# An expert layer over 256 tokens: 64 tokens by gathered rows, 192 by dense stages

## The chip, the cores and the metric

The kernel runs on one core of a Trainium2 chip. The metric is the device time of one execution in microseconds (us). The kernel before takes 3086.05 us (median of 3 runs, 3082.75 to 3087.93).

## What is computed

Two transformer blocks over 256 tokens of width 2048, in float32. The last layer is what the change touches: a product-key expert layer ("PEER"). Each of 8 heads of a token picks its 16 best of 16384 experts, so a token has 128 experts with a gate each; an expert is one row of `w_u` and one row of `w_v`, both of 2048 values.

```python
experts = e1 * PEER_KEYS + e2
gates = jax.nn.softmax(sc, axis=-1).astype(h.dtype)
...
    u = jnp.take(w_u, ib, axis=0)
    a = jnp.einsum('td,tkd->tk', hb, u)
    c = gb * jax.nn.gelu(a)
    vv = jnp.take(w_v, ib, axis=0)
    return jnp.einsum('tk,tkd->td', c, vv)
```

Its result is added to x, and a last RMS norm with a gain gives the output.

## The kernel before

Each engine has its own program, and semaphores join them. All weights come in items of 1 MB (128 partitions of 2048 values): SP loads item n into one of four slots of `raw` (L621) once item n-4 has been used; ScalarE rounds it to `w_hi` (L1361); VectorE subtracts to get `w_lo` (L2071); TensorE multiplies high and low parts, in the rounded format fp32r. Both splits run two items ahead of the matmuls.

The expert layer doesn't gather. It computes all 16384 experts for all 256 tokens and weighs them with a dense matrix of gates that is zero for experts not chosen. An item holds 128 experts. The experts are in four quarters of 32 items, and the stages follow each other as U0, U1, V0, U2, V1, U3, V2, V3; U is the product with `w_u`, V that with `w_v`.

- U0 (`activations`, L1220, q = 0): per item 16 blocks of 3 matmuls of 256 columns (the tokens). Meanwhile VectorE's `choose` (L2772) finds each token's experts.
- U1, U2, U3: per item 16 blocks of one matmul of 512 columns (high and low part of the tokens side by side, L1228) and one of 256 (L1232). VectorE adds the two halves (`add_halves`, L2905), ScalarE applies gelu (L1923), VectorE multiplies with the gates (`weigh_item`, L2899).
- U1 also makes the gates, 8 tokens per item: VectorE builds one-hot rows (`hots`, L2871 to L2878), TensorE multiplies them (`dense`, L1255), VectorE uses one quarter's gates (`weigh`, L2886), ScalarE keeps the other three (`keep`, L1935), and its queue sends them to memory (L1939). `fetch` brings them back in V0 and V1.
- V (`outputs`, L1259): per item 8 PSUM banks (2 halves of the tokens, 4 pieces of 512 columns), 3 matmuls of 512 columns each (L1274 to L1276). The stationary operand is the weighed activations of 128 tokens, as `c_hi` (ScalarE, L1955) and `c_lo` (VectorE, L2911). `c_hi` of an item waits until the item two before it has been used.

In V VectorE's order per item is `low_c` of the next item, then `split` of the one after it. In the tail VectorE adds the eight banks to x (L3006), ScalarE squares and sums (L2036), VectorE and ScalarE find the norm, and VectorE, ScalarE and GpSimd (L2057, its only work in the kernel) scale and send.

## Time and profile before

| | us |
|---|---|
| median of 3 runs | 3086.05 |
| shortest and longest run | 3082.75, 3087.93 |
| span of the profiled execution, first to last instruction | 3082.7 |
| expert stages, U0 to V3, within the span | 1600.7 to 3072.8 |

No time of the profiled execution is given beside its span; the span is within 0.1 us of the shortest run. In the rows below, PE is TensorE's matmuls, PEld its weight loads, DVE VectorE, ACT ScalarE, POOL GpSimd, SP the load queue; ACTq and SPq are queues that issue. A matmul's duration holds its way through the array, and matmuls overlap, so what one costs in a stream is the distance between two starts.

### The profile page before, as it was taken

The numbers are of one execution on the slowest core, as the hardware profiler recorded it, in microseconds if no ns is written. First come the engines' busy times: TensorE is split into PE (matmuls) and PEld (weight loads), VectorE is DVE, ScalarE is ACT, GpSimd is POOL, SyncE is SP. The second block draws the span as 40 slices with busy tenths as digits, with TensorE's granted clock in tenths as the row PEclk, the third lists the DMA queues.
The fourth block names the chain that finished last, engine by engine and source line by source line (L and its number), as shares of the span: only waits on it lengthen the run. The fifth ranks groups of instructions, "written<-read, shape, count | busy, mean of one in ns | idle before, by whom it ended". The sixth has DMA issues, their size and how long they took to land. (4 is left out here: it accounts for less than half of the span.)

```text
span 3082.7 us, 41075 instructions
## 1 busy us (share of the span) xinstructions
PE 2982.3 (97%) x16258; PEld 2568.4 (83%) x16258; DVE 1906.9 (62%) x2375; ACT 1360.0 (44%) x1511; POOL 5.3 (0%) x8
## 2 busy tenths in 40 slices
PE   7999989899998999999999999999999999999998
PEld 6888777789887888877899988878888888888887
DVE  4656675656586545464579988846565455554454
ACT  4544454444445443345535444444434443344444
POOL 0000000000000000000000000000000000000000
PEclk9999999999999999999999999999999999999999
DMA  6555534245453555444444555566555655555554
GB/s 240 180 196 186 194 131 174 73 168 182 153 194 108 178 184 189 154 158 155 141 163 180 188 186 206 206 235 226 213 187 203 232 193 188 190 191 191 206 195 157
DMA packets 97138, 560.56 MB, mean 182 GB/s; under 512 B 10888, under 2 KB 26880, under 8 KB 35328
## 3 DMA queue, kind: packets, MB, share of 16 engines
q1 hardware_dynamic: 73152, 522.03, 48.1%
q10 hardware_dynamic: 23872, 36.95, 3.4%
q8 instruction: 79, 1.29, 0.2%
q14 instruction: 35, 0.29, 0.0%
HBM read 543.15 MB, written 15.73 MB: 181 GB/s over the span
## 5 line engine op out<-in xcount | busy, mean ns | idle before, releaser
L2071 DVE TENSOR_TENSOR w_lo<-raw,w_hi 128x2048 fp32r<-128x2048 f32 (+2 forms) x500 | 1128.1, 2261 | 670.6 <-ACT w_hi L1361 664.8
L1361 ACT ACTIVATE w_hi<-raw 128x2048 fp32r<-128x2048 f32 (+2 forms) x500 | 940.8, 1888 | 397.8 <-DMA raw<-in_w_in_2.0 93.2
L767 PE MATMUL ps<-w_hi,hT 128*128 128x512 f32 (+3 forms) x1344 | 519.4, 386 | 12.0 <-DVE w_lo L2071 11.5
L769 PE MATMUL ps<-w_hi,hT 128*128 128x512 f32 (+3 forms) x1344 | 512.6, 381 | 0.0
L768 PE MATMUL ps<-w_lo,hT 128*128 128x512 f32 (+3 forms) x1344 | 512.4, 381 | 0.0
L1228 PE MATMUL ps<-hT,w_hi 128*128 128x512 f32 x1536 | 485.0, 397 | 0.5 <-issue 0.5
L1274 PE MATMUL ps<-w_hi,c_hi 128*128 128x512 f32 x1024 | 399.1, 390 | 4.0 <-DVE c_lo L2911 4.0
L1276 PE MATMUL ps<-w_hi,c_lo 128*128 128x512 f32 x1024 | 399.1, 390 | 0.0
L1275 PE MATMUL ps<-w_lo,c_hi 128*128 128x512 f32 x1024 | 399.0, 390 | 0.0
L1232 PEld LDWEIGHTS ps<-hT,w_lo 128*128 128x128 f32 x1536 | 288.6, 188 | 68.2
L767 PEld LDWEIGHTS ps<-w_hi,hT 128*128 128x128 f32 x1344 | 253.5, 189 | 59.5 <-DVE w_lo L2071 8.5
L1232 PE MATMUL ps<-hT,w_lo 128*128 128x256 f32 x1536 | 301.7, 278 | 0.0
L769 PEld LDWEIGHTS ps<-w_hi,hT 128*128 128x128 f32 x1344 | 253.5, 189 | 45.6
L768 PEld LDWEIGHTS ps<-w_lo,hT 128*128 128x128 f32 x1344 | 253.6, 189 | 44.0
L1228 PEld LDWEIGHTS ps<-hT,w_hi 128*128 128x128 f32 x1536 | 233.7, 189 | 0.9 <-issue 0.7
L1274 PEld LDWEIGHTS ps<-w_hi,c_hi 128*128 128x128 f32 x1024 | 192.6, 188 | 44.6 <-issue 3.7
L1276 PEld LDWEIGHTS ps<-w_hi,c_lo 128*128 128x128 f32 x1024 | 192.6, 188 | 40.0
L1275 PEld LDWEIGHTS ps<-w_lo,c_hi 128*128 128x128 f32 x1024 | 192.5, 188 | 40.0
L1955 ACT ACTIVATE c_hi<-work 128x256 fp32r (+1 forms) x128 | 53.4, 417 | 367.1 <-PE ps L1276 360.1
L1923 ACT ACTIVATE work<-work (+1 forms) x96 | 40.1, 418 | 318.4 <-DVE work L2905 318.4
L825 PE MATMUL ps<-w_hi,hT 128*128 128x512 f32 x384 | 154.5, 402 | 10.8 <-DVE hT L2174 10.6
L826 PE MATMUL ps<-w_lo,hT 128*128 128x512 f32 x384 | 152.0, 396 | 0.0
(274 smaller groups left out, 3418.3 us busy)
## 6 DMA issues: line engine op xcount, KB each, us to landing
raw<-in_w_u_t SPq DMA_DIRECT2D x128, 1024.0 KB, 4.8
raw<-in_w_v SPq DMA_DIRECT2D x128, 1024.0 KB, 5.3
raw<-in_w_in_2.0 SPq DMA_DIRECT2D x32, 1024.0 KB, 4.7
raw<-in_odd_w.0 SPq DMA_DIRECT2D x20, 1024.0 KB, 4.8
raw<-in_even_w.3608 SPq DMA_DIRECT2D x16, 1024.0 KB, 4.8
raw<-in_w_out.0 SPq DMA_DIRECT2D x16, 1024.0 KB, 4.8
raw<-in_w_out.1 SPq DMA_DIRECT2D x16, 1024.0 KB, 4.8
raw<-in_w_out_2.0 SPq DMA_DIRECT2D x16, 1024.0 KB, 4.8
```

What stands on the lines that cost most here:

```text
L767: pe.matmul(o, hi, wh, start=(j + k == 0), stop=False)
L768: pe.matmul(o, hi, wl, start=False, stop=False)
L769: mm = pe.matmul(o, lo, wh, start=False, stop=(j == 3 and k == 3))
L825: pe.matmul(o, hi, wh, start=begins and k == 0, stop=False)
L826: pe.matmul(o, hi, wl, start=False, stop=False)
L1228: pe.matmul(ps[:, s % 2, :], w_hi[:, s, k * P:(k + 1) * P], hT[:, k].rearrange("p n t -> p (n t)"), start=(k == 0), stop=False, skip_group ...
L1232: mm = pe.matmul(ps[:, s % 2, 0:S], w_lo[:, s, k * P:(k + 1) * P], hT_hi[:, k], start=False, stop=(k == KC - 1), skip_group_check=True)
L1274: pe.matmul(o, ch, wh, start=first and b in fresh, stop=False, skip_group_check=True)
L1275: pe.matmul(o, ch, wl, start=False, stop=False, skip_group_check=True)
L1276: mm = pe.matmul(o, cl, wh, start=False, stop=last and b in ends, skip_group_check=True)
L1361: act.activation(w_hi[:, s, 0:size], raw[:, s, 0:size], ACT.Copy).then_inc(hi_done, 1)
L2071: dve.tensor_tensor(w_lo[:, s, 0:size], raw[:, s, 0:size], w_hi[:, s, 0:size].bitcast(F32), ALU.subtract).then_inc(lo_done, 1)
```

## The change

Tokens 192 to 255 leave the dense expert stages. Their experts are gathered: GpSimd issues 128 indirect DMAs, each of 128 rows of 8 KB (two experts for each of the 64 tokens, one per partition), 64 from `w_u` and then 64 from `w_v`, into two buffers. VectorE multiplies each U row with the token's h and sums it, ScalarE applies gelu once to all, and VectorE adds each V row, weighed, to `YSUM`. Both run inside the loops of V0 to V3, 16 to 26 rows to a stage (`ROW_SHARE`). `YSUM` lies in the columns of `hT` that the 64 tokens leave.

The dense stages and the gates are for 192 tokens: U matmuls have 384 and 192 columns (192 in U0), the gates take 24 steps instead of 32. In V, the banks of the second half now hold 64 tokens only; their high and low parts lie side by side as one stationary operand of 128 columns, so two matmuls do instead of three. The two halves of such a bank, and `YSUM`, are joined at the end by f32 matmuls with a matrix of ones at pairs (`PAIRS`). VectorE's loops of these stages are written out instead of looped. The core of the diff:

```diff
+SG = 64
+SD = S - SG
...
+    c_parts = sb("c_parts", [P, 2, 2 * S], F32R)
+    c_hi, c_lo = c_parts[:, :, 0:S], c_parts[:, :, S:2 * S]
...
+    ROWS = [W(22880, D), W(18432, D)]
+    HROW, GROW = W(20832, D), W(22880, D)
+    YSUM = gaps[:, :, :, SD:S].rearrange("p k n t -> p (k n) t")
+    N_U, N_ROWS = P * SG // P, 2 * P * SG // P
+    PAIRS = W(20480, 2, P)
...
+                both_parts = ps[:, s % 2, 0:2 * SD].rearrange("p (n t) -> p n t", n=2)
                 for k0 in range(0, KC, 2):
                     for k in (k0, k0 + 1):
-                        pe.matmul(ps[:, s % 2, :], w_hi[:, s, k * P:(k + 1) * P],
-                                  hT[:, k].rearrange("p n t -> p (n t)"), start=(k == 0), stop=False,
-                                  skip_group_check=True)
+                        pe.matmul(both_parts, w_hi[:, s, k * P:(k + 1) * P], hT[:, k, :, 0:SD], start=(k == 0),
+                                  stop=False, skip_group_check=True)
                     for k in (k0, k0 + 1):
-                        mm = pe.matmul(ps[:, s % 2, 0:S], w_lo[:, s, k * P:(k + 1) * P], hT_hi[:, k], start=False,
-                                       stop=(k == KC - 1), skip_group_check=True)
+                        mm = pe.matmul(ps[:, s % 2, 0:SD], w_lo[:, s, k * P:(k + 1) * P], hT_hi[:, k, 0:SD],
+                                       start=False, stop=(k == KC - 1), skip_group_check=True)
                 mm.then_inc(item_used, 1)
...
+            banks = (2, 3, 4, 5, 6, 7, 0, 1) if first else END_BANKS if last and q > LASTU else range(8)
...
+                if b < 4:
+                    ch, cl = c_hi[:, s % 2, 0:P], c_lo[:, s % 2, 0:P]
+                    pe.matmul(o, ch, wh, start=begins, stop=False, skip_group_check=True)
+                    pe.matmul(o, ch, wl, start=False, stop=False, skip_group_check=True)
+                    mm = pe.matmul(o, cl, wh, start=False, stop=ends_, skip_group_check=True)
+                else:
+                    c2 = c_parts[:, s % 2, P:S]
+                    pe.matmul(o, c2, wh, start=begins, stop=False, skip_group_check=True)
+                    mm = pe.matmul(o, c2, wl, start=False, stop=ends_, skip_group_check=True)
...
+        with pe.Fori(0, STEPS // RAW) as i:
             for s in range(RAW):
                 activations(i, s, 1)
                 dense(i, s)
-        for s in range(RAW - 1):
-            activations(LOOPS - 1, s, 1)
-            dense(LOOPS - 1, s)
-        dense(LOOPS - 1, RAW - 1)
-        activations(LOOPS - 1, RAW - 1, 1)
+        with pe.Fori(STEPS // RAW, LOOPS) as i:
+            for s in range(RAW):
+                activations(i, s, 1)
         for q in range(PARTS):
...
+        pe.wait_ge(fin_in, 32)
+        pe.wait_ge(row_used, N_ROWS)
+        for n in range(4):
+            pe.wait_ge(fin_add, n + 1)
+            pe.matmul(ps[:, 4 + n, :], PAIRS[:, 0], x[:, 1, n * 512:(n + 1) * 512], start=True, stop=False)
+            pe.matmul(ps[:, 4 + n, :].rearrange("p (a t) -> p a t", t=SG), PAIRS[:, 1], YSUM[:, 8 * n:8 * n + 8],
+                      start=False, stop=True).then_inc(joined, 1)
...
+        pool.wait_ge(h_ready, 1)
+        pool.dma_start(HROW[0:SG], HROW[SG:P]).then_inc(h_in, 16)
+        pool.wait_ge(evac_act, pq_act0 + 4)
+        pool.tensor_copy(YSUM[SG:P], x[SG:P, 1].rearrange("p (a t) -> p a t", t=SG)).then_inc(y_set, 1)
+        pool.memset(YSUM[0:SG], 0.0).then_inc(y_set, 1)
+        pool.wait_ge(y_set, 2)
+        pool.memset(x[SG:P, 1], 0.0).then_inc(y_set, 1)
+        pool.wait_ge(picked, 2)
+        pool.dma_start(gsm[0:SG, 0], gsm[SG:P, 2]).then_inc(pick_in, 16)
+        pool.wait_ge(pick_in, 16)
+        for n in range(N_ROWS):
+            if n == 1:
+                for b in range(2):
+                    pool.wait_ge(gates_out[b], 16 + 16 * STEPS // 2)
+            if n >= 2:
+                pool.wait_ge(row_used, n - 1)
+            k = n % N_U
+            pool.indirect_dma_start(ROWS[n % 2], None, A["w_u_rows"] if n < N_U else A["w_v_2"][0],
+                                    bass.IndirectOffsetOnAxis(ap=PICKS[:, k:k + 1].bitcast(U32), axis=0)
+                                    ).then_inc(row_in[n % 2], 16)
+        pool.wait_ge(fin_in, 32)
+        for b in range(2):
...
+            c = CTS[q % 2][:, 4 * i + s]
+            dve.tensor_tensor(c_lo[:, s % 2, 0:P], c[:, 0:P], c_hi[:, s % 2, 0:P].bitcast(F32), ALU.subtract)
+            dve.tensor_tensor(c_parts[:, s % 2, SD:S], c[:, P:SD], c_hi[:, s % 2, P:SD].bitcast(F32), ALU.subtract
+                              ).then_inc(c_lo_done, 1)
...
+        def rows():
+
+            dve.wait_ge(h_in, 16)
+            for n in range(N_U):
+                dve.wait_ge(row_in[n % 2], 16 * (n // 2 + 1))
+                dve.tensor_tensor_reduce(ROWS[n % 2], ROWS[n % 2], HROW, 1.0, 0.0, ALU.mult, ALU.add,
+                                         AROW[:, n:n + 1]).then_inc(row_used, 1)
+                yield
+            dve.wait_ge(row_gelu, 1)
+            dve.tensor_tensor(CROW, CROW, PICK_OF, ALU.mult).then_inc(row_c, 1)
+            dve.wait_ge(row_c, 1)
+            dve.wait_ge(y_set, 3)
+            for n in range(N_U, N_ROWS):
+                dve.wait_ge(row_in[n % 2], 16 * (n // 2 + 1))
+                dve.wait_ge(row_used, n)
+                dve.scalar_tensor_tensor(out=YSUM, in0=ROWS[n % 2].rearrange("p (a t) -> p a t", t=SG),
+                                         scalar=CROW[:, n - N_U:n - N_U + 1], in1=YSUM, op0=ALU.mult, op1=ALU.add
+                                         ).then_inc(row_used, 1)
+                yield
+
+        rowing = rows()
+        ROW_SHARE = {("V", 0): 24, ("U", 2): 16, ("V", 1): 24, ("U", 3): 16, ("V", 2): 26, ("V", 3): 22}
+
+        def take_rows(part, m):
+
+            n, of = ROW_SHARE[part], QTR - 2
+            for _ in range(min(m + 1, of) * n // of - min(m, of) * n // of):
+                next(rowing)
 
         def weave():
 
-            def step(i, s, last=False):
-                ends = last and s == RAW - 1
-                if not ends:
...
+            hots(0)
+            for m in range(QTR):
+                i, s = m // RAW, m % RAW
+                if m + 1 < STEPS:
+                    hots(m + 1)
                 u_split(i, s, 1)
...
+                if m < STEPS:
...
+            for m in range(QTR):
+                i, s = m // RAW, m % RAW
                 u_split(i, s, q)
...
+                take_rows(("U", q), m)
...
+            for m in range(QTR):
+                i, s = m // RAW, m % RAW
+                v_step(i, s, i == LOOPS - 1)
+                if q == 0 and 3 <= i < 5:
+                    if m == 3 * RAW:
+                        dve.wait_ge(gates_in, 16 * PIECES)
+                        dve.wait_ge(gelu_done, 2 + 2 * QTR)
+                    weigh_four(i - 3, s)
+                take_rows(("V", q), m)
...
+        def joined_gain(n):
+            dve.wait_ge(fin_sum, 4 + n + 1)
+            dve.tensor_tensor(XG1[:, n * 512:(n + 1) * 512], ps[:, 4 + n, :], GFIN[:, n * 512:(n + 1) * 512], ALU.mult
+                              ).then_inc(fin_g, 1)```

Left out are the smaller shapes of the gate tables, the order of the banks in the last item (4 to 7 first), the tail's order of sums, two more loads (`GROW`, `PAIRS`) on ScalarE's queue, and this, early in the key projection on VectorE:

```diff
+                if g == 0 and j == 3:
+                    dve.scalar_tensor_tensor(out=HROW[SG:P], in0=x[SG:P, 1], scalar=sm(NR + 1)[SG:P], in1=GROW[SG:P],
+                                             op0=ALU.mult, op1=ALU.mult).then_inc(h_ready, 1)
...
+            if q == PARTS - 1:
+                act.wait_ge(row_used, N_U)
+                act.activation(CROW, AROW, ACT.Gelu_apprx_tanh).then_inc(row_gelu, 1)
```

## Rows read from the trace of the kernel before

**Rows 1.** Page, part 1: busy time, share of span, instructions.

```profile
PE 2982.3 (97%) x16258; PEld 2568.4 (83%) x16258; DVE 1906.9 (62%) x2375; ACT 1360.0 (44%) x1511; POOL 5.3 (0%) x8
```

**Rows 2.** Stages U0 to V3, tail: stretch, length, busy by engine, clock, DMA share, GB/s.

```profile
1600.70:1786.40 185.70, 185.22 (x1542) 184.99 (x1542) 164.68 (x334) 93.90 (x83) 0.00 (x0) 1.00 0.49 176
1786.40:2017.30 230.90, 224.97 (x1792) 200.55 (x1792) 199.51 (x203) 97.38 (x96) 0.00 (x0) 1.00 0.58 201
2017.30:2193.20 175.90, 175.82 (x769) 145.42 (x770) 96.85 (x74) 73.25 (x65) 0.00 (x0) 0.99 0.68 237
2193.20:2371.90 178.70, 178.48 (x1026) 155.59 (x1024) 105.24 (x95) 70.97 (x64) 0.00 (x0) 1.00 0.53 188
2371.90:2546.00 174.10, 174.10 (x768) 144.16 (x769) 89.06 (x68) 72.00 (x65) 0.00 (x0) 1.00 0.63 217
2546.00:2724.60 178.60, 178.59 (x1026) 155.63 (x1024) 105.00 (x94) 71.16 (x64) 0.00 (x0) 1.00 0.53 188
2724.60:2898.50 173.90, 173.69 (x766) 143.88 (x767) 88.01 (x68) 71.61 (x65) 0.00 (x0) 1.00 0.55 194
2898.50:3072.80 174.30, 174.30 (x770) 144.33 (x769) 86.44 (x70) 72.79 (x73) 3.38 (x3) 1.00 0.52 180
3072.80:3082.70 9.90, 0.41 (x2) 0.00 (x0) 4.37 (x9) 4.63 (x11) 1.71 (x2) 0.69 0.52 212
```

**Rows 3.** Waits in V1: who waited for whom, us, times, longest.

```profile
ACT c_hi L1955 <- PE ps L1276: 92.9, 30, 3.3
DVE w_lo L2071 <- ACT w_hi L1361: 42.0, 31, 2.3
```

**Rows 4.** Timelines (start, duration); by-line rows (durations min/median/max): V0, U0, f32.

```profile
2185.69 0.39 PE L1274 MATMUL ps<-w_hi,c_hi 128*128 128x512 f32 x1
...
2192.95 0.39 PE L1276 MATMUL ps<-w_hi,c_lo 128*128 128x512 f32 x1
...
1699.83 0.28 PE L1240 MATMUL ps<-hT,w_hi 128*128 128x256 f32 x1
...
1702.95 0.28 PE L1242 MATMUL ps<-hT,w_lo 128*128 128x256 f32 x1
...
1539.37 1.95 PE L1183 MATMUL ps<-work 128*128 128x128 f32 x16
...
794.98 1.89 PE L1072 MATMUL ps<-work 128*128 128x256 f32 x8
...
L1183 PE MATMUL ps<-work x64: 272/275/348, 1539.4 to 1599.4; 128*128 128x128 f32 x64
...
L968 PEld LDWEIGHTS ps<-w_hi,c_hi x64: 106/108/173, 372.1 to 418.7; 128*32 128x32 f32 x64
...
L1274 PEld LDWEIGHTS ps<-w_hi,c_hi x1024: 186/188/330, 2017.3 to 3072.1; 128*128 128x128 f32 x171
```

**Rows 5.** By line, from 1800 us: busy, mean ns, idle before and releaser.

```profile
L2071 DVE TENSOR_TENSOR w_lo<-raw,w_hi 128x2048 fp32r<-128x2048 f32 x221 | 506.6, 2292 | 344.6 <-ACT w_hi L1361 344.6
...
L2911 DVE TENSOR_TENSOR c_lo<-work,c_hi 128x256 fp32r<-128x256 f32 x128 | 54.4, 425 | 147.0 <-ACT c_hi L1955 146.9
...
L3025 DVE SCALAR_TENSOR_TENSOR x<-x,small,work 128x1024 f32<-128x1024 f32 x2 | 2.6, 1289 | 0.1
```

**Rows 6.** DMA: two stretches of the first loads; issues, KB each, us to landing.

```profile
12.00:14.00 2.00, 2.00 (x11) 2.00 (x10) 0.00 (x0) 1.99 (x5) 0.00 (x0) 1.00 1.01 426
20.00:22.00 2.00, 1.65 (x4) 1.39 (x5) 2.00 (x6) 2.00 (x2) 0.00 (x0) 0.50 1.06 444
...
raw<-in_w_v SPq DMA_DIRECT2D x128, 1024.0 KB, 5.3
...
x<-in_x SPq DMA_DIRECT2D x2, 1024.0 KB, 13.4
```

**Rows 7.** Timeline of U1, VectorE's `weigh` of two items in a row.

```profile
1981.33 0.41 DVE L2886 TENSOR_TENSOR work<-work,ps 128x256 f32 x1
...
1988.19 0.41 DVE L2886 TENSOR_TENSOR work<-work,ps 128x256 f32 x1
```

More of the change, by code:

```diff
@@ L89, in tables @@
     out["pool"] = np.ascontiguousarray(pool.reshape(NT, P, 4, S).transpose(1, 0, 2, 3))
+    pairs = np.zeros((P, 2, P), f)
+    for i in range(P):
+        pairs[i, 0, i % SG] = 1.0
+        pairs[i, 1, SG + i % SG] = 1.0
+    out["pairs"] = pairs
     out["iota"] = np.tile(np.arange(P, dtype=f)[None], (P, 1))
@@ L125, in build_in @@
     raw = nc.alloc_sbuf_tensor_at("raw", [P, RAW, 2048], F32, offset=RAW_AT)
-    c_hi = sb("c_hi", [P, 2, S], F32R)
-    c_lo = sb("c_lo", [P, 2, S], F32R)
+    gaps = nc.alloc_sbuf_tensor_at("gaps", [P, KC, 2, S], F32, offset=GAPS_AT)
+    c_parts = sb("c_parts", [P, 2, 2 * S], F32R)
+    c_hi, c_lo = c_parts[:, :, 0:S], c_parts[:, :, S:2 * S]
     WORK = 24928
@@ L194, in build_in @@
     fin_add = sem("fin_add")
+    h_ready = sem("h_ready")
+    h_in = sem("h_in")
+    y_set = sem("y_set")
+    picked = sem("picked")
+    pick_in = sem("pick_in")
+    row_in = [sem(f"row_in{b}") for b in range(2)]
+    row_used = sem("row_used")
+    row_gelu = sem("row_gelu")
+    row_c = sem("row_c")
+    joined = sem("joined")
+    fin_g = sem("fin_g")
     fin_mul = sem("fin_mul")
@@ L539, in build_in @@
     STEPS = S // TG
-    CTS = [W(QTR * S * q, QTR, S) for q in range(2)]
-    E1T = W(19936, S)
-    E2T = W(20192, S)
-    GT = W(20448, S)
-    IOTA = W(20704, P)
+    STEPS = SD // TG
+    CTS = [W(QTR * SD * q, QTR, SD) for q in range(2)]
+    E1T = W(20064, S)
+    E2T = W(20320, S)
+    GT = W(20576, S)
     def WB(off, *shape):
@@ L1859, in _ @@
         load(IOTA, A["iota"])
+        load(GROW, A["ffn_row"].partition_broadcast(P))
         for j in range(2):
@@ L1954, in high @@
                 act.wait_ge(weighed, PIECES + 2 * QTR)
-            act.activation(c_hi[:, s % 2], CTS[q % 2][:, bass.ds(4 * i + s, 1)].rearrange("p a t -> p (a t)"),
+            if q == 0 and isinstance(i, int) and i + s == 0:
+                act.wait_ge(gate_used, 2 + STEPS)
+            act.activation(c_hi[:, s % 2, 0:SD], CTS[q % 2][:, bass.ds(4 * i + s, 1)].rearrange("p a t -> p (a t)"),
                            ACT.Copy).then_inc(c_hi_done, 1)
         def u_part(q):
-            with act.Fori(0, LOOPS - 1) as i:
+            if q == PARTS - 1:
+                act.wait_ge(row_used, N_U)
+                act.activation(CROW, AROW, ACT.Gelu_apprx_tanh).then_inc(row_gelu, 1)
+            if q == 1:
+                with act.Fori(0, STEPS // RAW) as i:
+                    for s in range(RAW):
+                        u_split(i, s, q)
+                        activate(i, s, q)
+                        keep(i, s)
+            with act.Fori(STEPS // RAW if q == 1 else 0, LOOPS - 1) as i:
                 for s in range(RAW):
@@ L2920, in step @@
                 u_split(i, s, 1)
-                if ends:
-                    weigh(i, s)
+                if m == QTR - 1:
                     low_c(0, 0, 0)
                 add_halves(i, s, 1)
-                if not ends:
+                if m < STEPS:
                     weigh(i, s)
-            hots(0, 0)
-            with dve.Fori(0, LOOPS - 1) as i:
-                for s in range(RAW):
-                    step(i, s)
-            for s in range(RAW):
-                step(LOOPS - 1, s, True)
@@ L2935, in u_part @@
         def u_part(q):
-            def step(i, s, last=False):
+            dve.wait_ge(gates_in, 16 * PIECES * q)
+            for m in range(QTR):
+                i, s = m // RAW, m % RAW
                 u_split(i, s, q)
-                if last and s == RAW - 1:
+                if m == QTR - 1:
                     low_c(0, 0, q - 1)
                 add_halves(i, s, q)
-                if s > 0:
-                    weigh_item(i, s - 1, q)
-                elif not isinstance(i, int) or i > 0:
-                    weigh_item(i - 1, RAW - 1, q)
@@ L2947, in u_part @@
-            dve.wait_ge(gates_in, 16 * PIECES * q)
-            for s in range(RAW):
-                step(0, s)
-            with dve.Fori(1, LOOPS - 1) as i:
-                for s in range(RAW):
-                    step(i, s)
-            for s in range(RAW):
-                step(LOOPS - 1, s, True)
+                if m > 0:
+                    weigh_item((m - 1) // RAW, (m - 1) % RAW, q)
+                take_rows(("U", q), m)
             weigh_item(LOOPS - 1, RAW - 1, q)
         dve.drain().then_inc(sums_done, 1)
+        dve.scalar_tensor_tensor(out=gsm[SG:P, 0:3:2, 0:SG].bitcast(U32),
+                                 in0=KEYS[SG:P, 1, 0].rearrange("p (a k) -> p a k", a=2), scalar=float(E1),
+                                 in1=KEYS[SG:P, 1, 1].rearrange("p (a k) -> p a k", a=2), op0=ALU.mult, op1=ALU.add
+                                 ).then_inc(picked, 1)
```

168 lines of the change are left out of this document (78 added, 90 removed).

## Prediction

> **What bounds the kernel now.** I read the shares of the span first: matmuls fill 97% of 3082.7 us, VectorE 62%, ScalarE 44% [rows 1]. A share near 100% over stages with different limits says little, so I cut the span at the first matmul of each expert stage [rows 2]: U0 185.7 us, U1 230.9, then V0 175.9, U2 178.7, V1 174.1, U3 178.6, V2 173.9, V3 174.3, and 9.9 us of tail. From V0 on PE is busy in over 99.8% of every stage, while VectorE works 86 to 105 us of some 175: these stages are TensorE's. In U1 and U0 VectorE is nearly as full (199.5 of 230.9 and 164.7 of 185.7), which limits what a faster TensorE can give there. The waits of V1 agree: ScalarE's c_hi waits 92.9 us for the matmuls of the item before, and VectorE's split 42.0 us for ScalarE [rows 3]. That idle VectorE time is what the change fills.
>
> Next, what one matmul costs, as the distance between starts. [rows 4]: 512 columns, 32 steps in 7.26 us, 0.227 us each; 256 columns, 26 steps in 3.12 us, 0.120 each. So a column costs (0.227 - 0.120)/256 = 0.00042 us, and 0.013 is left per matmul. An item (1 MB of experts) is then 24 x 0.227 = 5.45 us in V, 48 x 0.1205 = 5.78 in U0, 16 x (0.227 + 0.120) = 5.56 in the other U stages; [rows 2] divided by 32 gives 5.43 to 5.50, 5.80 and 5.58.
>
> **The profiled execution** has no time of its own beside its span. 3082.7 us agrees with the shortest run shown (3082.75); the median, 3086.05, is 3.3 above. I sum against the span and add 3.3.
>
> **The change, part by part.**
>
> *V matmuls.* Banks 4 to 7 take two matmuls instead of three: 20 x 0.227 = 4.54 us per item on PE.
>
> *U matmuls.* The wide ones go to 384 columns: 0.227 - 128 x 0.00042 = 0.174 us. The narrow ones go to 192, and no such fp32r matmul is in the trace. Below: by columns alone 0.094. Above: nothing gained, 0.120. The nearest row in between is an f32 stream of 128 columns with a 128-column weight load each, 16 in 1.95 us, 0.112 per step ((1.95 - 0.275)/15, with the median duration of that row) [rows 4]. Weight loads last 188 ns for 128 columns and 108 for 32 [rows 4], so 0.83 ns per column, 0.107 us of loading that a 192-column matmul (0.080 of columns) no longer covers. I take 0.112: U0 48 x 0.112 = 5.38 us per item, the others 16 x (0.174 + 0.112) = 4.58 (4.29 to 4.70).
>
> *VectorE per item.* 2.292 us at 2048 elements and 0.425 at 256 [rows 5] give 1.042 ns per element and 0.158 fixed. c_lo in two pieces (128 and 64) is 0.29 + 0.22 = 0.51; add_halves at 384 is 0.56, weigh_item at 192 is 0.36. A U row, a product with a sum at 2048, is taken as the split, 2.29; a V row (scalar_tensor_tensor) as 1.289 at 1024 elements [rows 5] plus 1024 x 1.042 ns, 2.36. I use 2.36 for both (2.3 to 2.5). Rows per stage are 24, 16, 24, 16, 26, 22 over 32 items. So VectorE needs per item: V0 0.51 + 2.29 + 1.77 + 0.24 (eight weigh_four) = 4.81; V1 4.57; V2 4.72; V3 4.42; U2 and U3 2.29 + 0.56 + 0.36 + 1.18 = 4.39.
>
> *Bytes.* A gather is 128 rows of 8 KB, 1.05 MB, as much as an item. V0 moves 32 + 24 of these and 16 fetches of gates (0.52 MB): 67.1 MB; V1 62.9, V2 60.8, V3 56.6. The highest rate the trace shows is 426 to 444 GB/s, in the first loads [rows 6]; at 430 that is 4.88 us per item in V0, 4.57, 4.42 and 4.11.
>
> So in V three resources stand within some 7% of each other: 4.54 for PE, 4.4 to 4.8 for VectorE, 4.1 to 4.9 for the transfers. The larger of the three per stage is 4.88, 4.57, 4.72, 4.54: 32 x 18.71 = 599 us. U1, where PE and VectorE are close today, loses 230.9/225.0 - 1 = 2.6% of PE's busy time to waits [rows 2]; with a third resource I take 5%: 629 us against 698.2 [rows 2], **-69** (bounds 581, PE alone, and 708, the rival "transfers").
>
> *Where the rows wait.* A row stands in VectorE's queue behind low_c and split of an item. A late gather therefore holds up the next c_lo and split, and TensorE behind them, after the little slack of one item. ScalarE's gelu of CROW waits for row 64, and GpSimd's last gain products stand behind the last gather. GpSimd issues gather n once row n-2 is used, so two buffers turn in (L + 2.36)/2 us per row, L from issue to landing. No gather is in the trace. Below: a 1 MB load beside little else, 5.3 us; above: one queued behind others in the crowded start, 13.4 [rows 6]. I take 8, nearer the first, since at most two transfers share the engines most of the time: 5.2 us per row, against 32 x 4.9/26 = 6.0 wanted in V2. Hidden, but not by much. At 13.4 it would be 7.9 x 128 = 1009 us for V0 to V3.
>
> *U2, U3.* PE 4.58, VectorE 4.39, 48 transfers per 32 items at 430 GB/s 3.7: I take 4.65, 149 us each against 178.6: **-59** (-40 to -80).
>
> *U1.* 24 of 32 items keep the gate matmuls. PE is busy 225.0 us there, 7.03 per item [rows 2], so the gates cost 7.03 - 5.58 = 1.45 and PE would need 4.58 + 1.45 = 6.03. But a loop between VectorE and ScalarE is next: weigh, keep, its DMA issue, ScalarE's split, VectorE's split, add_halves, weigh again, 1981.33 to 1988.19, 6.86 us [rows 7]. It shrinks by 0.13 (add_halves) and 0.05 (gelu): 6.68. 24 x 6.68 + 8 x 4.6 + 5.9 (today's remainder) = 203: **-28** (-5 to -43, the latter if PE's 6.03 sets it).
>
> *U0.* PE offers 32 x 0.4 = 13; VectorE's choice of experts is for all 256 tokens still and needs 164.7 us [rows 2]. I take **-10** (0 to -21).
>
> *Tail.* After the last output, PE joins halves and rows: 8 f32 matmuls of 512 columns. The 256-column f32 row gives at most 1.89/8 = 0.236 per record, two records per matmul [rows 4], so 4 x 0.236 = 0.94 for 512 columns and 7.6 us in all, against the adds and squares that they replace on the path: **+4** (0 to +9).
>
> *Taken as nothing:* HROW's product (2.36 us, VectorE, in the key projection) and GROW's load, covered by the weight stages ahead of U0, +3 at most if not; GpSimd's copies and memsets, on an engine idle until the tail [rows 1]; SP's loads, whose number and order stay; ScalarE's two extra issues and the gelu of CROW, since row 64 is V1's last (24 + 16 + 24).
>
> Sum: -10 - 28 - 69 - 59 + 4 = **-162**; 3082.7 - 162 + 3.3 = **2924 us**.
>
> **The rivals.**
>
> *Narrow matmuls.* Slower than before. Place: the 3072 fp32r matmuls of 192 columns. For it: no row shows fp32r under 256 columns, and f32 costs 0.223 us for 128 columns (two records of 0.112), 1.74 ns per column. At that price 192 columns are 0.335: U0 48 x (0.335 - 0.1205) x 32 = +329, U2 and U3 16 x (0.174 + 0.335) = 8.14 per item, +164, U1 8.14 + 1.45 = 9.59 for 24 items and 8.14 for 8, +70; with V and tail -65: about 3584. It outweighs the gain from about 0.174 us on. Against it: 256 columns run at the same rate as 512. Chance 0.15.
>
> *Gather turnaround.* From L = 12.1 on, 64 x (L + 2.36) exceeds the 927 us that V0 to V3 take above; from L = 14.7 the kernel is slower than before. At 14: 1047 us, 3044. For it: GpSimd builds each list of rows itself, and VectorE now almost never rests. Against it: twelve us is more than twice the 5.3 of today's loads. The Trainium skill, "SBUF — State Buffer", Who interferes with whom, says that a VectorE instruction with two SBUF inputs shuts out a GpSimd one that reads SBUF until it ends; every split and row is of that kind, so by that rule L grows by up to one such instruction. No run here shows it. Chance 0.19: 0.09 faster still, 0.02 same, 0.08 slower.
>
> *Transfers.* V0 moves 237 GB/s at a share of 0.68 of the engines' time [rows 2], so 237/0.68 = 349 at a full share. If that is the ceiling for weights and gathers together, V takes 192 + 180 + 174 + 162 = 708 us, and the time is 2924 + 79 = 3003. Against it: 426 to 444 GB/s in the first loads [rows 6], though those had no second stream. Chance 0.09. The Trainium skill, "DMA: Bandwidth & Descriptors", Specifications, gives about 358 GB/s of HBM per core as the limit; by that, V would be 691 us and the sum 2986, an estimate from the page, which the first loads of this trace exceed by 19% or more.
>
> The forecast itself has 0.57, with a range of its own of 2855 to 3000.
>
> **How the numbers follow.** About 0.2% is what a measurement of this kernel can tell from no change. Faster: 0.57 + 0.09 + 0.09 = 0.75; slower: 0.15 + 0.08 = 0.23; the same 0.02. The range starts at the forecast's lower bound and goes to 3150, which takes in the turnaround up to L = 15.6; the narrow-matmul case is left out, and some of either tail.
>
> **What would show it.** Starts of U0's matmuls 0.112 apart confirm the price of 192 columns; 0.094 or 0.17 and more refute it. V items at 4.9 us with VectorE over 90% busy and PE waiting now and then for c_lo or w_lo confirm the balance; VectorE idle for gathers in front of the rows names turnaround; loads landing in 8 us and more at 360 GB/s name the transfers. U1's period of 6.7 confirms its loop. The prediction is wrong if V stays at 5.4, or if U0 grows.

## The result and the profile after

The changed kernel takes 3033.43 us (median of 4 runs, 3028.62 to 3041.34) against 3085.78 for the kernel before (4 runs): a ratio of 0.983, 95% interval 0.9815 to 0.985. It is 52 us faster where 162 was forecast; the time lies in the range that was given, the sign is right, but of the two largest of the five terms of the sum, V0 to V3 did not come at all and U2 and U3 came by less than half. The profiled execution took 3036.65 us, its span is 3034.8.

Part 1 of the page, of the changed kernel:

```profile
PE 2817.5 (93%) x15570; PEld 2445.3 (81%) x15570; DVE 2133.7 (70%) x2671; ACT 1345.7 (44%) x1504; POOL 255.6 (8%) x139
```

TensorE's busy time fell by 165 us against [rows 1], about as much as the forecast wanted of the time, and the span by 48: TensorE now waits. Where it waits stands in the same windows as [rows 2], U0 to V3 and the tail:

```profile
1598.70:1773.60 174.90, 173.17 (x1543) 172.44 (x1543) 164.73 (x334) 92.19 (x83) 2.22 (x2) 1.00 0.52 187
1773.60:1985.70 212.10, 189.75 (x1600) 184.69 (x1600) 169.89 (x174) 89.43 (x88) 4.21 (x3) 0.98 0.62 218
1985.70:2161.90 176.20, 157.74 (x641) 124.57 (x642) 144.91 (x153) 71.36 (x64) 24.37 (x24) 0.95 0.93 358
2161.90:2328.30 166.40, 153.23 (x1026) 148.64 (x1024) 131.27 (x129) 70.11 (x64) 43.29 (x16) 1.00 0.81 309
2328.30:2505.10 176.80, 157.78 (x641) 124.43 (x642) 138.40 (x147) 71.61 (x65) 24.23 (x24) 0.95 0.91 346
2505.10:2670.80 165.70, 152.69 (x1026) 148.49 (x1024) 132.21 (x114) 70.11 (x64) 43.10 (x16) 0.99 0.81 309
2670.80:2845.00 174.20, 152.20 (x623) 120.69 (x624) 139.63 (x122) 69.89 (x65) 60.10 (x26) 0.96 0.91 335
2845.00:3020.10 175.10, 158.28 (x659) 125.25 (x658) 136.12 (x125) 71.56 (x68) 47.94 (x22) 0.97 0.85 313
3020.10:3034.80 14.70, 7.05 (x17) 2.85 (x15) 6.42 (x14) 7.07 (x19) 1.91 (x2) 0.86 0.35 143
```

| stage | before | after | difference | forecast |
|---|---|---|---|---|
| U0 | 185.7 | 174.9 | -10.8 | -10 |
| U1 | 230.9 | 212.1 | -18.8 | -28 |
| V0 to V3 | 698.2 | 702.3 | +4.1 | -69 |
| U2 and U3 | 357.3 | 332.1 | -25.2 | -59 |
| tail | 9.9 | 14.7 | +4.8 | +4 |

(Ahead of U0 the changed kernel is 2 us shorter; over the kernels below, with the same code there, U0 starts between 1598.7 and 1604.7 us, so these 2 us are not told from nothing.) In V, TensorE idles 17 to 22 us of each stage; VectorE is busy 78 to 82% of it, the DMA engines 85 to 93%. No one resource is full.

Who waits there, in V0 of the changed kernel (engine, line, releaser: us in total, times, longest), then the weights' issues of 1990 to 2155 us with their median time to landing:

```profile
ACT w_hi L1402 <- DMA raw<-in_w_v: 63.8, 25, 6.3
PE ps L1306 <- DVE c_parts L3000: 18.3, 13, 3.3
DVE work L3008 <- DMA work<-in_w_u_rows,gsm: 7.7, 6, 2.4
...
raw<-in_w_v SPq DMA_DIRECT2D x28, 1024.0 KB, 9.3
```

In the kernel before, the same view of V0 had this:

```profile
ACT w_hi L1361 <- DMA raw<-in_w_v: 16.2, 12, 2.3
```

ScalarE now waits 63.8 us there for weights, which land in 9.3 us instead of 5.3 [rows 6]. Not all of that wait costs time: without any rows (below) ScalarE still waits 42.2 us for weights in V0, while TensorE never idles. VectorE waits little for gathers in V0, but in V2 of the changed kernel more:

```profile
ACT w_hi L1402 <- DMA raw<-in_w_v: 49.0, 25, 4.7
PE ps L1306 <- DVE c_parts L3000: 27.3, 15, 5.3
DVE gaps L3018 <- DMA work<-in_w_v,gsm: 20.2, 14, 2.3
```

In U2 the timeline shows another thing, the same every 5.1 to 5.2 us, in items with a row and without:

```profile
2204.49 0.55 DVE L2991 TENSOR_REDUCE work<-ps 128x192 f32<-128x384 f32 x1
...
2205.18 0.36 ACT L1965 ACTIVATE work<-work  x1 [2.92 <-DVE work L2991]
...
2205.53 1.92 ACT L1402 ACTIVATE w_hi<-raw 128x2048 fp32r<-128x2048 f32 x1
...
2207.48 2.29 DVE L2153 TENSOR_TENSOR w_lo<-raw,w_hi 128x2048 fp32r<-128x2048 f32 x1
...
2209.69 0.55 DVE L2991 TENSOR_REDUCE work<-ps 128x192 f32<-128x384 f32 x1
```

add_halves of one item releases gelu (0.36), ScalarE's next split stands behind that gelu (1.92), VectorE's split behind ScalarE's (2.29), and the next add_halves behind VectorE's split in its queue. That is a ring of 0.55 + 0.36 + 1.92 + 2.29 = 5.12 us per item, more than TensorE's 4.6. The order was the same in the kernel before, under 5.58 us of matmuls per item.

So there are two questions: which of transfers, VectorE's time and the turn of the two buffers holds V, and whether the ring holds U2 and U3.

### The profile page after: what moved, and what is told of

It reads as the page before. It is cut to its first block, busy times and chain, and to the rows that moved or that the text cites. A ratio compares the mean times of both kernels' runs of the same rounds, so it can differ in the third digit from the quotient of the medians.

```text
span 3034.8 us, 39269 instructions
## 1 busy us (share of the span) xinstructions
PE 2817.5 (93%) x15570; PEld 2445.3 (81%) x15570; DVE 2133.7 (70%) x2671; ACT 1345.7 (44%) x1504; POOL 255.6 (8%) x139
## 4 chain that ended last, share of the span: by engine, by line
PE 53%; DVE 23%; DMA 11%; ACT 8%; issue 3%; ACTq 2%; DVEq 0%; SPq 0%
DVE w_lo L2153 10%; PE ps L796 9%; PE ps L798 9%; PE ps L797 9%; ACT w_hi L1402 6%; DMA raw<-in_w_v 5%; PE ps L854 3%; DMA work<-in_w_v,gsm 3%; PE ps L856 3%; PE ps L855 3%; DVE gaps L3018 2%; DVE work L3008 2%; DMA work<-in_w_u_rows,gsm 2%; PE ps L1306 2%; PE ps L1308 2%
## 5 line engine op out<-in xcount | busy, mean ns | idle before, releaser
L2153 DVE TENSOR_TENSOR w_lo<-raw,w_hi 128x2048 fp32r<-128x2048 f32 (+2 forms) x500 | 1129.1, 2263 | 507.9 <-ACT w_hi L1402 501.2
L1402 ACT ACTIVATE w_hi<-raw 128x2048 fp32r<-128x2048 f32 (+2 forms) x500 | 942.1, 1891 | 615.4 <-DMA raw<-in_w_v 239.2
L1258 PE MATMUL ps<-hT,w_hi 128*128 128x384 f32 x1536 | 419.7, 354 | 29.6 <-DVE work L2991 29.1
L1306 PE MATMUL ps<-w_hi,c_parts 128*128 128x512 f32 x512 | 215.8, 421 | 91.8 <-DVE c_parts L3000 86.5
L1261 PEld LDWEIGHTS ps<-hT,w_lo 128*128 128x128 f32 x1536 | 278.8, 188 | 0.0
L1261 PE MATMUL ps<-hT,w_lo 128*128 128x192 f32 x1536 | 278.5, 263 | 0.0
L1306 PEld LDWEIGHTS ps<-w_hi,c_parts 128*128 128x128 f32 x512 | 100.8, 197 | 138.3 <-DVE c_parts L3000 84.0
L1307 PE MATMUL ps<-w_lo,c_parts 128*128 128x512 f32 x512 | 208.6, 407 | 0.0
L1308 PE MATMUL ps<-w_hi,c_parts 128*128 128x512 f32 x512 | 208.4, 407 | 0.0
L1311 PE MATMUL ps<-w_hi,c_parts 128*128 128x512 f32 x512 | 202.5, 396 | 0.1
L1312 PE MATMUL ps<-w_lo,c_parts 128*128 128x512 f32 x512 | 201.2, 393 | 0.0
L2132 POOL DMA_INDIRECT work<-in_w_v,gsm x64 | 152.4, 2382 | 359.9 <-DVE gaps L3018 350.7
L3018 DVE SCALAR_TENSOR_TENSOR gaps<-work,gsm,gaps 128x2048 f32<-128x2048 f32 x64 | 150.3, 2348 | 29.3 <-DMA work<-in_w_v,gsm 29.2
L1965 ACT ACTIVATE work<-work (+1 forms) x96 | 35.0, 364 | 289.1 <-DVE work L2991 289.1
## 6 DMA issues: line engine op xcount, KB each, us to landing
raw<-in_w_u_t SPq DMA_DIRECT2D x128, 1024.0 KB, 4.8
raw<-in_w_v SPq DMA_DIRECT2D x128, 1024.0 KB, 7.4
raw<-in_w_in_2.0 SPq DMA_DIRECT2D x32, 1024.0 KB, 4.7
raw<-in_odd_w.0 SPq DMA_DIRECT2D x20, 1024.0 KB, 4.9
raw<-in_even_w.3608 SPq DMA_DIRECT2D x16, 1024.0 KB, 4.9
raw<-in_w_out.0 SPq DMA_DIRECT2D x16, 1024.0 KB, 4.9
raw<-in_w_out.1 SPq DMA_DIRECT2D x16, 1024.0 KB, 4.8
raw<-in_w_out_2.0 SPq DMA_DIRECT2D x16, 1024.0 KB, 4.8
```

Source lines behind the costliest of these rows:

```text
L1258: pe.matmul(both_parts, w_hi[:, s, k * P:(k + 1) * P], hT[:, k, :, 0:SD], start=(k == 0), stop=False, skip_group_check=True)
L1261: mm = pe.matmul(ps[:, s % 2, 0:SD], w_lo[:, s, k * P:(k + 1) * P], hT_hi[:, k, 0:SD], start=False, stop=(k == KC - 1), skip_group_check=True)
L1306: pe.matmul(o, ch, wh, start=begins, stop=False, skip_group_check=True)
L1307: pe.matmul(o, ch, wl, start=False, stop=False, skip_group_check=True)
L1308: mm = pe.matmul(o, cl, wh, start=False, stop=ends_, skip_group_check=True)
L1402: act.activation(w_hi[:, s, 0:size], raw[:, s, 0:size], ACT.Copy).then_inc(hi_done, 1)
```

## The experiments

Lengths of the stages in us, cut at the first matmul of each; V2 and V3 together run to the start of the first matmul of their last bank. Every kernel below "halves first" contains its edit.

| kernel | time | U1 | V0 | U2 | V1 | U3 | V2+V3 |
|---|---|---|---|---|---|---|---|
| before | 3085.8 | 230.9 | 175.9 | 178.7 | 174.1 | 178.6 | 347.5 |
| changed | 3033.4 | 212.1 | 176.2 | 166.4 | 176.8 | 165.7 | 348.6 |
| no rows | 2919.9 | 212.5 | 147.5 | 163.8 | 147.2 | 163.9 | 291.3 |
| products only | 2940.0 | 212.2 | 157.6 | 164.4 | 150.6 | 165.5 | 294.2 |
| quarter gathers | 2965.4 | 212.2 | 163.1 | 165.0 | 156.5 | 166.0 | 309.4 |
| short products | 2982.9 | 212.3 | 164.6 | 167.8 | 164.0 | 167.2 | 315.6 |
| unconnected | 3004.5 | 212.2 | 173.4 | 165.4 | 170.8 | 166.1 | 324.3 |
| halves first | 2986.8 | 186.5 | 178.3 | 147.2 | 175.5 | 148.3 | 354.2 |
| + spread | 2952.8 | 186.4 | 170.8 | 148.9 | 168.1 | 150.1 | 332.5 |
| + three buffers | 2957.1 | 186.5 | 179.4 | 148.4 | 172.9 | 148.1 | 328.0 |
| + contiguous | 2965.6 | 186.5 | 174.7 | 147.9 | 177.7 | 147.3 | 337.3 |
| + row before split | 2975.0 | 186.5 | 177.3 | 147.9 | 173.1 | 147.3 | 348.3 |
| joined | 2917.5 | 186.5 | 166.3 | 149.3 | 162.4 | 152.1 | 305.3 |
| joined, U1 rows | 2910.1 | 188.1 | 160.1 | 149.1 | 160.8 | 150.9 | 307.9 |

Times without an interval below are of one run each, beside a kernel before at 3084.2 to 3085.9. How far one run can be trusted is seen where a stage's code is the same: V0 takes 176.2, 178.3 and 179.4 us in changed, halves first and three buffers, V1 176.8, 175.5 and 172.9, and V2 and V3 348.6 and 354.2 in the first two. Differences of up to some 4 us in a V stage, or 6 in V2 and V3 together, are not told from no change.

**No rows.**

```
-        for n in range(N_ROWS):
+        for n in range(0):
...
-        ROW_SHARE = {("V", 0): 24, ("U", 2): 16, ("V", 1): 24, ("U", 3): 16, ("V", 2): 26, ("V", 3): 22}
+        ROW_SHARE = {(a, q): 0 for a in "UV" for q in range(PARTS)}
```

(and without TensorE's and ScalarE's waits for rows and the gelu of `CROW`).

> Left out: the experts of the 64 tokens that get rows (no gathers and no row products; the dense stages are for the other 192 tokens as in the changed kernel). All theories of the V stages (transfers, turnaround of the two buffers, VectorE's time) expect TensorE's 4.54 us per item here: 145 to 148 us for each of V0 to V3 against 174 to 177 in the changed kernel. For U2 and U3 two theories differ: if the loop of add_halves, gelu, ScalarE's split and VectorE's split sets the period (5.1 us by the trace), they stay at 162 to 166 us without a single row; if VectorE's rows or the gathers set it, they fall to 147 to 150 (TensorE's 4.6 per item). Time about 3033 - 4 x 29 = 2917 in the first case, 2885 in the second.

Its V0 and U2:

```profile
1989.00:2136.50 147.50, 147.50 (x640) 121.90 (x641) 91.21 (x105) 71.56 (x64) 0.00 (x0) 0.98 0.76 263
2136.50:2300.30 163.80, 152.40 (x1025) 148.34 (x1024) 97.64 (x97) 70.01 (x64) 0.00 (x0) 0.99 0.59 212
```

V is TensorE's without rows, 4.6 us per item: the matmuls were priced rightly, and the 29 us per V stage are all due to the rows. U2 stays at 163.8 with VectorE busy 60% and the DMA engines 59%: neither rows nor gathers hold it. The ring does.

**Products only.** The gathers are gone; the first half's products read the scaled activations, the second half's whatever lies in the buffers.

```
-                dve.wait_ge(row_in[n % 2], 16 * (n // 2 + 1))
-                dve.tensor_tensor_reduce(ROWS[n % 2], ROWS[n % 2], HROW, 1.0, 0.0, ALU.mult, ALU.add,
+                dve.tensor_tensor_reduce(ROWS[n % 2], HROW, HROW, 1.0, 0.0, ALU.mult, ALU.add,
...
-        for n in range(N_ROWS):
+        for n in range(0):
```

(and without the second half's wait for gathers).

> Left out: the gathers; the 128 row products stand where they stood in VectorE's order, on data that lie in SBUF, so the 64 tokens' outputs mean nothing. Transfers, turnaround and the lock on GpSimd all expect the V stages to fall to 147 to 154 us each (VectorE's 4.8 per item at most). VectorE's time (rows of 2.3 us ahead of the next low_c and split) expects 165 or more, up to the 174 to 177 of the changed kernel.

VectorE's time alone costs 10.1 us in V0 (3.6 over the bound given), 3.4 in V1 and 2.9 in V2 and V3; the last two are within what one run cannot tell. As the main cause it falls.

**Short products.**

```
-                dve.tensor_tensor_reduce(ROWS[n % 2], ROWS[n % 2], HROW, 1.0, 0.0, ALU.mult, ALU.add,
+                dve.tensor_tensor_reduce(ROWS[n % 2][:, 0:SG], ROWS[n % 2][:, 0:SG], HROW[:, 0:SG], 1.0, 0.0, ALU.mult, ALU.add,
```

(and the same cut in the second half's product).

> Left out: 31/32 of each row product (64 of 2048 columns); all gathers as in the changed kernel. Transfers expect the V stages to stay at 168 us or more: the same bytes go through the same engines. Turnaround expects (9.3 + 0.2)/2 = 4.75 us per row or less, since the lock of a long VectorE instruction also goes, and so about 150 us per V stage (2930 in all). VectorE's time expects 146 to 150.

V0 of this kernel:

```profile
1986.40:2151.00 164.60, 152.18 (x641) 119.98 (x642) 94.40 (x152) 68.48 (x64) 22.49 (x24) 0.99 0.95 381
```

Neither bound was met (168 from below, 150 from above). With next to no products, the gathers alone cost 17.1, 16.8 and 24.3 us over "no rows", some 60% of what the rows cost in V0 and V1. The DMA engines are busy 95% and move 381 GB/s, not 430. A gather lands in 9.6 us here (median), so the two buffers turn in (9.6 + 0.2)/2 = 4.9 us per row, just under the 164.6/32 = 5.1 of an item. But VectorE still waits 15.6 us for gathers in V0, so the 17.1 us are what the gathers cost, not surely their bytes alone.

**Quarter gathers.** As many descriptors, each a quarter as long; the first half's products take both inputs from the activations, at full length and still behind their gathers.

```
-            pool.indirect_dma_start(ROWS[n % 2], None, A["w_u_rows"] if n < N_U else A["w_v_2"][0],
+            pool.indirect_dma_start(ROWS[n % 2][:, 0:512], None, (A["w_u_rows"] if n < N_U else A["w_v_2"][0]).rearrange("e (b d) -> (e b) d", b=4),
```

> Left out: three quarters of each gathered row (128 rows of 2 KB instead of 8 KB, as many gathers and descriptors, and all products at full length and behind their gathers). Transfers expect the V stages at 147 to 154 us (44 MB instead of 63 in V0). Turnaround expects the same or a little more, since a short gather also lands sooner ((5 + 2.4)/2 = 3.7 us per row). VectorE's time, or the lock on the issue alone, expects 160 or more.

V0 163.1 is where VectorE's time or the lock had expected it, V1 156.5 lies between the two. Three quarters of the bytes gone give back 13 to 20 us of the 29 in V0 and V1 and 39 of 57 in V2 and V3. So the length of the gathers makes about two thirds of the cost in V1, V2 and V3 but less than half in V0 (13.1 of 28.7), and what is left (15.6 us in V0, 9.3 in V1) is more than the products alone cost. A shorter gather also lands sooner, so this run does not part the bytes from the turn of the buffers.

**Unconnected.**

```
-                pool.wait_ge(row_used, n - 1)
+                pool.wait_ge(row_in[n % 2], 16 * (n // 2))
+                pool.wait_ge(item_used, at[n - 2])
...
-                dve.wait_ge(row_in[n % 2], 16 * (n // 2 + 1))
```

Both halves' products have the second half's form here (2.35 us) and read the scaled activations.

> Left out: the connection of gathers and products. All 128 gathers are issued at the items of the changed kernel and all 128 products run at full length, but the products read data that lie in SBUF and wait for no gather, and a gather waits for the landing of the one two before and for its item, not for a product. With short products the V stages took about 164 us against 176, so transfers carry some 17 of the 29 us and long products the rest. If the rest is VectorE's in-order wait for late gathers, V falls to 160 to 166 here; if it is VectorE's time or the lock that a long VectorE instruction puts on the gather's issue, it stays at 172 to 178.

173.4, 170.8 and 324.3: against the changed kernel the connection itself costs 2.8 us in V0, 6.0 in V1, and 24.3 in V2 and V3. So in V0 the in-order wait for late gathers is not the main cost, as expected of VectorE's time or of the lock; in V2 and V3 it holds. But GpSimd is busy 52.9 us with its 24 issues in V0 here, against 24.4 in the changed kernel: here issues are held up that go through there, so the connection can cost V0 more than the 2.8. V0 of this kernel:

```profile
1987.30:2160.70 173.40, 155.49 (x640) 121.58 (x641) 144.88 (x130) 70.84 (x64) 52.87 (x24) 0.97 0.93 369
```

The excess over "no rows" is 25.9, 23.6 and 33.0 us, and the sum of products alone and of gathers with short products is 27.2, 20.2 and 27.2. **The costs add up**, within what one run can tell, instead of the largest one hiding the others.

**Halves first.**

```
-                u_split(i, s, q)
                 if m == QTR - 1:
                     low_c(0, 0, q - 1)
                 add_halves(i, s, q)
                 if m > 0:
                     weigh_item((m - 1) // RAW, (m - 1) % RAW, q)
+                u_split(i, s, q)
```

(and the same in U1: add_halves and weigh ahead of the split).

> Nothing left out: in the U stages VectorE adds the halves of an item (and weighs) before it splits the item two ahead, so that ScalarE's next split no longer stands behind a gelu that waits for VectorE's split. If the loop of add_halves, gelu and the two splits sets the period of U2 and U3 (5.1 us), they fall from 166 to 149 to 154 us each, and U1 from 212 to about 198 to 203 (24 items at 6.1 to 6.3); about 2992 us in all, V as it was. If the transfers set U2 and U3 (309 GB/s at a share of 0.81), they stay at 160 or more.

Two weigh instructions in a row of U1, first in the changed kernel, then with halves first; and U2 with halves first:

```profile
1875.99 0.41 DVE L2972 TENSOR_TENSOR work<-work,ps 128x256 f32<-128x256 f32 x1
...
1882.76 0.41 DVE L2972 TENSOR_TENSOR work<-work,ps 128x256 f32<-128x256 f32 x1
```

```profile
1851.38 0.42 DVE L2972 TENSOR_TENSOR work<-work,ps 128x256 f32<-128x256 f32 x1
...
1857.39 0.42 DVE L2972 TENSOR_TENSOR work<-work,ps 128x256 f32<-128x256 f32 x1
...
2144.40:2291.60 147.20, 146.96 (x1026) 146.78 (x1024) 128.84 (x128) 71.66 (x64) 15.04 (x16) 1.00 0.92 338
```

U2 and U3 fall to TensorE's 4.6 us per item and U1 to 186.5 us, all below the expected ranges; U1's period is 6.01, the 6.03 that the prediction gave as TensorE's own need. The order of three instructions on VectorE was worth 47 us, nearly as much as the whole change. V hardly moved (+2.1, -1.3, +5.6). At a DMA share of 0.92, U2 is not slowed, so a high share does not by itself say that a stage is held by its transfers.

**Spread.**

```
-        ROW_SHARE = {("V", 0): 24, ("U", 2): 16, ("V", 1): 24, ("U", 3): 16, ("V", 2): 26, ("V", 3): 22}
+        ROW_SHARE = {("V", 0): 22, ("U", 2): 20, ("V", 1): 22, ("U", 3): 20, ("V", 2): 22, ("V", 3): 22}
```

> Nothing left out: the U stages' order of halves_first, and the rows spread as 22, 20, 22, 20, 22, 22 over V0, U2, V1, U3, V2, V3 instead of 24, 16, 24, 16, 26, 22. If the transfers set V and still leave room in U2 and U3 (0.92 of the engines' time there), each of the 8 rows taken from V saves about 1.1 us there (28 us for 24 rows) and costs nothing in U: 2977 to 2980 us in all against 2986.8. If U2 and U3 are now at the transfers' limit too, they grow by 3 to 5 us each and the sum stays at 2984 to 2990.

More than either expected: 8 rows fewer in V gave 36.6 us, 3.7 each in V0 and V1 and 5.4 in V2, and cost 3.5 in U. The average row costs 1.2 us (28.7 for 24); the last ones cost three to four and a half times as much (against the changed kernel's V stages, 2.7 us each in V0 and 4.0 in V2). That they bring the pace near the turn of the buffers is a reading that was not tested.

**Three buffers.**

```
-    ROWS = [W(22880, D), W(18432, D)]
+    ROWS = [W(22880, D), W(18432, D), W(20832, D)]
...
-                pool.wait_ge(row_used, n - 1)
+                pool.wait_ge(row_used, n - 1 if n < N_U + 2 else n - 2)
```

> Nothing left out: halves_first, and from row 64 on a third buffer for gathered rows (the scaled activations' place, which no row reads after row 63). Turnaround with VectorE's in-order wait expects what separates the unconnected kernel from the connected one in V2 and V3 (24 us of 349) to go for the most part: V2 and V3 at 328 to 340 us against 354, 2963 to 2975 in all; V0 and V1 as they were. Transfers alone expect V2 and V3 unchanged within 4 us, since the bytes are the same.

V2 and V3 fall by 26.2 us to 328.0 (20.6 against the changed kernel), V0 stays (+1.1). VectorE's waits for gathers there, 35.7 us with halves first, are gone from the view; ScalarE's for weights grow. First halves first, then three buffers, V2 and V3:

```profile
ACT w_hi L1402 <- DMA raw<-in_w_v: 107.8, 49, 5.4
...
DVE gaps L3018 <- DMA work<-in_w_v,gsm: 35.7, 18, 4.7
```

```profile
ACT w_hi L1404 <- DMA raw<-in_w_v: 133.2, 57, 4.8
```

**Contiguous.**

```
-        vv = A["w_v_2"][0].rearrange("(r c) d -> c r d", c=E1)
+        vv = A["w_v_t"]
```

> Nothing left out: halves_first, and the dense V stages load their items from a copy of the table in which an item's 128 rows lie side by side (as the U stages' copy does), instead of rows 1 MB apart. If the spacing holds the transfers to 360 to 380 GB/s, V falls by 5 to 9% of its 176 us (160 to 168 us each, 2945 to 2965 in all); if the engines' own limit does, V stays within 3 us.

Inconclusive: V2 and V3 fall by 16.9 us, V0 by 3.6, and V1 rises by 2.2; neither V0 nor V1 comes near 168. The changes of V0 and V1 are within what one run cannot tell. The spacing seems to cost something in V2 and V3; why V1 does not gain was not followed up.

**Row before split.**

```
+                take_rows(("V", q), 4 * i + s)
                 if not (last and (s >= 2 and q == PARTS - 1 or s == 3 and q != LASTU)):
                     split(i + (v_first[q] // 4 + (s + 2) // 4), (s + 2) % 4, 2048)
```

> Nothing left out: halves_first, and in the V stages a row stands between low_c and the split in VectorE's order instead of behind the split. A late gather then holds up the split of the item two ahead (one item of slack more) and no longer the next c_lo. If TensorE's waits for c_lo (some 44 us in each of V0, V1 and 100 in V2 and V3, counting engine and weight loads) come from that order, V falls by 5 us or more per stage (2955 to 2970 in all); if the transfers set the pace, c_lo's waits only turn into waits for w_lo and the time stays at 2980 to 2990.

V falls by 1.0, 2.4 and 5.9 us, less than expected of the order and within what one run cannot tell, in a total between the two expectations. So the order of these two is at most a small part; TensorE's wait for c_lo is where the lateness shows.

**Joined, and joined with rows in U1.** The first has all four edits; the second also takes 5 rows in U1's last items:

```
                 u_split(i, s, 1)
+                if m in (25, 27, 28, 30, 31):
+                    next(rowing)
```

> Nothing left out: halves_first with the four changes together (rows spread 22, 20, 22, 20, 22, 22; a third buffer from row 64 on; the contiguous copy for the dense V stages; a row ahead of the split). Alone the first three gave 34, 30 and 21 us. If they remove different waits, they add up to 2905 to 2925; if they all relieve the one queue of transfers, the last ones give little: 2930 to 2945.

> Nothing left out: the joined kernel with 5 rows moved into the last 7 items of U1 (which have no gates; VectorE has 1.7 us per item to spare there), and 19, 19, 21, 20, 22, 22 behind. If V0 is still held by its bytes (gates and rows), it loses 3 rows at 1.1 to 3.7 us each: 4 to 10 us less than the joined kernel. If U1 pays for them (its end is TensorE's at 4.6 per item), no difference within 3 us.

2917.53 us (2910.51 to 2919.84), ratio 0.9454 (0.9438 to 0.9469); and 2910.08 (2908.16 to 2920.27), ratio 0.9442 (0.9423 to 0.9462). Alone the four edits gave 33.9, 29.6, 21.2 and 11.8 us over halves first, 96.5 together; joined they give 69, the middle of the first expectation: most of what they save adds up, about a quarter does not. The second is 7 us lower by its median, within the 4 to 10 expected, but the intervals overlap, so the gain of the U1 rows is not shown. Both beat the kernel before by 5.5% and the changed one by 4%. V0 and U2 of the last:

```profile
1964.90:2125.00 160.10, 150.38 (x640) 120.28 (x641) 135.75 (x146) 70.53 (x64) 50.86 (x20) 0.99 0.97 383
2125.00:2274.10 149.10, 147.78 (x1026) 147.13 (x1024) 136.73 (x134) 71.94 (x64) 17.82 (x19) 1.00 0.94 353
```

V0 now stands at about the 380 GB/s of short products, which suggests that what is left there is the transfers'; no run tried it.

## Why the prediction was right and wrong

**Right: U0 and the tail.** Starts in U0 lie 0.112 us apart ((1692.80 - 1689.78)/27), which settles the rival of narrow matmuls, and the sum of U0 is right to 1 us. In the tail TensorE is busy 7.05 us, where 7.6 had been worked out for its joins:

```profile
1689.78 0.27 PE L1271 MATMUL ps<-hT,w_lo 128*128 128x192 f32 x1
...
1692.80 0.27 PE L1271 MATMUL ps<-hT,w_lo 128*128 128x192 f32 x1
```

**Nearly right: U1.** The period of 6.77 is the loop's 6.68 that was worked out. But the last 8 items were put at TensorE's 4.6, and the ring of the other U stages holds them at 5.0 (add_halves at 1965.23 and 1970.23 us). That is 3 of the 9 us missing; the rest is loop time over 6.68 and what lies between the stages.

**Wrong: U2 and U3, -59.** The failed step is "PE 4.58, VectorE 4.39, 48 transfers per 32 items at 430 GB/s 3.7: I take 4.65". It compared engines' sums and left out the ring of 5.12 us that passes through two engines in order, though a like ring was drawn for U1 one paragraph further. "No rows" shows it (163.8 us without a row), "halves first" removes it (-18.3 us a stage against the changed kernel). With the ring cut, 147.2 and 148.3 us stand where 149 was forecast.

**Wrong: V, -69.** The failed step is "The larger of the three per stage" with 5% for waits. In V0 the three resources do not hide one another: products alone add 10.1 us, gathers with short products 17.1, both unconnected 25.9, connected 28.7. Within that step 430 GB/s was mis-sized too: it is a rate of single 2-us stretches, and the mean of V0 with next to no products is 381. The bytes were put somewhat too high: the change also shortens the fetches of gates, and V0 moves 358 GB/s x 176.2 us = 63 MB, not 67.1. So the gathers take V0 to 164.6 us (short products), where the forecast had 32 x 4.88 = 156 for the transfers, and the products' 10.1 us on top make 174.7 of the 176.2 measured.

Why they come on top can be read from the trace, though no run tried it by itself. The trips of an item through the DMA engines, ScalarE, VectorE and TensorE form another ring: SP loads an item when the item four before it has been used. In V0 of the changed kernel (means of items 5 to 32) a load lands after 8.7 us, the two splits take 1.9 and 2.3, and a row's share, `low_c` and the matmuls 1.77 + 0.51 + 4.54: 19.7 us in all, where four items at TensorE's rate are 4 x 4.54 = 18.2. Without rows the same sum is 6.4 + 1.9 + 2.3 + 0.51 + 4.54 = 15.7. So by this estimate the ring alone asks for 19.7/4 = 4.9 us per item, 158 us in V0, and a later landing and a row in VectorE's queue both lengthen it. That is not the whole of the 176.

The Trainium skill, "DMA: Bandwidth & Descriptors", Specifications, gives about 358 GB/s of HBM per core, and the changed kernel's V0 stands at just that; but the 381 and 383 of two experiments pass it, so the page's figure is not what stops V0.

**The rivals.** "Transfers" gave V 708 us, and 702.3 were measured, but not for its reason: 349 GB/s is no ceiling, since shorter products alone lift V0 to 381; that its 708 lies so near is luck. The time of the kernel lies in the stated range only because the range reached up to 3150 for the turnaround. "Gather turnaround" is seen in V2 and V3 at a price of some 25 us (the connection's 24.3, the third buffer's 26.2), though far from its L of 12. In the timeline of V2 (start, duration):

```profile
2748.09 2.69 POOL L2132 DMA_INDIRECT work<-in_w_v,gsm  x1 [3.74 <-DVE gaps L3018]
...
2753.93 2.28 DVE L2153 TENSOR_TENSOR w_lo<-raw,w_hi 128x2048 fp32r<-128x2048 f32 x1
...
2753.95 3.08 POOL L2132 DMA_INDIRECT work<-in_w_v,gsm  x1 [3.17 <-DVE gaps L3018]
...
2757.36 2.35 DVE L3018 SCALAR_TENSOR_TENSOR gaps<-work,gsm,gaps 128x2048 f32<-128x2048 f32 x1 [1.14 <-DMA work<-in_w_v,gsm]
...
2767.32 0.94 POOL L2132 DMA_INDIRECT work<-in_w_v,gsm  x1 [4.26 <-DVE gaps L3018]
```

The gather issued at 2748.09 is used at 2757.36: L is 9.3 (8 had been taken), and two buffers turn in (9.3 + 2.35)/2 = 5.8 us per row. V2 needs a row every 174.2/26 = 6.7 us on average, but most of them in successive items of 174.2/32 = 5.4 us, sooner than the buffers turn; and with nothing stored up a late row is never made good.

**The stated tests.** V stayed at 5.5 us per item, which had been named as refuting the forecast, with VectorE at 82% in V0 and not over 90; weights landing in 9.3 us pointed to the transfers, 20.2 us of waits for gathers in V2 to the turnaround. Both pointed right, each for a part.

## What to carry to other kernels

Where several resources of a stage come within some 10% of one another, don't take the largest: add what each costs over the bound, or look for the slack (items ahead, buffers) that would let one hide the other. Before crediting a shorter engine time, follow for every stage one item round through all engines, in the order of their queues; the ring that was hidden is the next bound, and re-ordering two instructions may break it. Here the last rows that fill a stage cost several times the average, so spread such work over stages and leave some slack.
